# Prompt attention: value products on half the array each, four at once, and softmax sums from the row pass

## The reference, cut to what matters

```python
def fox_block(qi, cq, qpos, k, v, ck):
    scale = FOX_DIM ** -0.5                                   # FOX_DIM = 64, SEQ = 2048, 8 heads
    logits = jnp.einsum('bqhd,bkhd->bhqk', qi, k, preferred_element_type=jnp.float32) * scale
    logits = logits + cq[..., :, None] - ck[..., None, :]     # c: running sum of the log forget values
    mask = jnp.arange(k.shape[1])[None, :] <= qpos[:, None]
    logits = jnp.where(mask, logits, -jnp.inf)
    p = jax.nn.softmax(logits, axis=-1).astype(v.dtype)
    return jnp.einsum('bhqk,bkhd->bqhd', p, v)
```

## Time and profile before

| | |
|---|---|
| Median of 3 runs | 3781.91 us (3779.85 to 3783.17) |
| Profiled execution, own time | 3778.13 us |
| Its span | 3776.4 us |
| TensorE busy | 3628.9 us, 96% |
| VectorE busy | 1614.3 us, 43% |
| ScalarE busy | 1170.2 us, 31% |
| Mean granted TensorE clock | 0.988 of 2.4 GHz |

### The profile page before, as it was taken

How to read it: one execution, slowest core, us unless ns; L and a number is a source line. 1 busy time by engine, 2 the same in 40 slices (tenths; PEclk the granted TensorE clock), 3 DMA queues, 4 the chain that set the end, 5 groups by cost and what they waited for, 6 DMA issues and landing times. The chain is left out here.

```text
span 3776.4 us, 54542 instructions
## 1 busy us (share of the span) xinstructions
PE 3628.9 (96%) x20888; PEld 3168.2 (84%) x20888; DVE 1614.3 (43%) x3505; ACT 1170.2 (31%) x2318; POOL 337.4 (9%) x416
## 2 busy tenths in 40 slices
PE   8999999899999999998879999999999999999998
PEld 8999999777777677776668889999999999888886
DVE  4000377655554554444544444444444444432222
ACT  5122122334333333332223333333333333321111
POOL 3000000211211111121200000000000000000000
PEclk9999999999999999999979999999999999999999
DMA  4212322311221022015443421111111111432222
GB/s 158 70 62 64 83 73 70 91 29 43 58 51 40 25 62 47 19 55 179 162 153 121 129 72 44 46 46 46 46 46 46 46 46 35 153 126 81 81 81 68
DMA packets 328132, 278.90 MB, mean 74 GB/s; under 512 B 97219, under 2 KB 292915, under 8 KB 326894
## 3 DMA queue, kind: packets, MB, share of 16 engines
q1 hardware_dynamic: 318319, 258.03, 23.0%
q0 software_dynamic: 5216, 18.23, 1.4%
q10 hardware_dynamic: 4416, 0.14, 0.1%
HBM read 190.70 MB, written 85.65 MB: 73 GB/s over the span
## 5 line engine op out<-in xcount | busy, mean ns | idle before, releaser
L2627 PE MATMUL bank<-ffn_hn_hi,ffn_w_parts 128*128 128x436 f32 (+1 forms) x3520 | 986.4, 361 | 2.4 <-ACTq L2734 2.4
L2627 PEld LDWEIGHTS bank<-ffn_hn_hi,ffn_w_parts 128*128 128x128 f32 x3520 | 661.3, 188 | 39.1 <-issue 2.7
L2627 PE MATMUL bank<-ffn_hn_lo,ffn_w_parts 128*128 128x436 f32 (+1 forms) x1760 | 634.1, 360 | 0.0
L416 PE MATMUL bank<-in_xh,in_wh 128*128 128x436 f32 (+1 forms) x1280 | 356.4, 359 | 2.3 <-DVE in_wh L634 2.3
L2627 PEld LDWEIGHTS bank<-ffn_hn_lo,ffn_w_parts 128*128 128x128 f32 x1760 | 330.8, 188 | 19.3
L2661 PE MATMUL bank<-ffn_down_wa,ffn_g_hi 128*128 (+1 forms) x1224 | 328.6, 390 | 3.4 <-DVE ffn_g_lo L2956 3.4
L2763 ACT COPY ffn_raw<-bank 128x436 f32<-128x436 f32 (+1 forms) x220 | 110.3, 501 | 704.2 <-PE bank L2627 649.7
L1555 PE MATMUL bank<-heads_p_pT,heads_p_v 128*65 128x512 f32 (+3 forms) x640 | 286.4, 529 | 10.3 <-issue 9.8
L2890 DVE TENSOR_SCALAR ffn_hist<-ffn_raw 128x2 f32 (+2 forms) x264 | 44.9, 170 | 547.7 <-ACT ffn_acc L2767 544.9
L2661 PEld LDWEIGHTS bank<-ffn_down_wa,ffn_g_hi 128*128 128x128 f32 x1224 | 229.9, 188 | 52.7 <-DVE ffn_down_wa L2953 3.3
L1612 ACT ACTIVATE heads_p_pT<-bank 128x512 f32<-128x512 f32 (+1 forms) x320 | 170.1, 533 | 271.4 <-PE bank L1540 170.0
(11 more groups left out here) (419 smaller groups left out, 6232.5 us busy)
## 6 DMA issues: line engine op xcount, KB each, us to landing
ffn_w<-in_w_up_dram SPq DMA_DIRECT2D x44, 512.0 KB, 5.0
ffn_g_raw<-scratch_g SPq DMA_DIRECT2D x110, 192.0 KB, 2.3
scratch_g<-ffn_acc SPq DMA_DIRECT2D x88, 218.0 KB, 2.0
heads_s_k<-in_cache_fox_k_dram SPq DMA_DIRECT2D x8, 2048.0 KB, 13.5
heads_s_v<-in_cache_fox_v_dram SPq DMA_DIRECT2D x8, 2048.0 KB, 8.3
heads_d_qkvT<-scratch_gch SPq DMA_DIRECT2D x17, 768.0 KB, 5.6
ffn_y<-in_w_down_dram SPq DMA_DIRECT2D x22, 512.0 KB, 3.4
scratch_gch<-in_work SPq DMA_DIRECT2D x48, 218.0 KB, 1.9
```

What stands on the lines that cost most here:

```text
L416: mm = pe.matmul(bank[:, 4 + i % 2, 0:wide], a[:, k, :], b[:, k, col:col + wide], start=(k == 0 and m == 0), stop=(k == KD - 1 and m == 2))
L2627: mm = pe.matmul(bank[:, pair(n) + e, 0:width], w_parts[a][:, part, e, k, :], x[:, k, cols], start=(k == 0 and m == 0), stop=(k == KD - 1 ...
```

## The change

**Values.** `v` loses its column of ones and has 64 columns. The product of an even key block goes to PSUM partitions 0 to 63 and that of an odd block to partitions 64 to 127 of the same bank, so each uses 64 of the array's columns. `values_tensor` now issues four products in a row (`AT_ONCE`), after the fourth block's exponential. `pT` has eight buffers instead of three (`NPT`); they are lent by `Delta.S_s`, the running streams' states, whose load on SP now waits until the last row-bank use of `Prompt` is freed. `oT` has 128 rows; `turn_out` transposes 128x128 pieces, and `normalise` adds the two halves with a reduction over the turned bank before it multiplies. (In the first piece of a head only the even half has been written, so 64 rows are turned.)

**Sums.** The softmax denominator is taken from the row pass. The operands `q_both`, `q_hi`, `causal` and the exponentials' scale change sign, so that a tile's row minimum is the negated maximum and can serve as ScalarE's bias. After `row_max`, ScalarE exponentiates the same tile from PSUM into a scratch tile `junk`, with `accum_out` as its row sum, and frees the bank. `sums_vector` and `sums_scalar` (between its first two steps, `share = exp(rise)`) weigh the tiles' sums by exp of their distance to the group's maximum and take the reciprocal.

**Waits and times.** `row_free` becomes two semaphores, one for each bank. `SPEED` goes from 0.62 to 0.54 and the block's cost in `set_times` from 2.65e-3 to 1.81e-3 a column; `Prompt.end` goes from 974.9 to 897.6 units (the sum of `cost(G) / SPEED` over the 32 groups, plus 34.0), while `Delta`'s times stay. The last scaling of `Sample` on VectorE gets a due time 10.2 units later.

```diff
@@ Delta.sync
             if t == NC - 2:
+                sp.wait_ge(*self.prompt.freed(len(self.prompt.uses) - 1))
                 sp.dma_start(self.S_s[:].rearrange("p b h n -> p (b h) n"),
@@ Prompt
-    SPEED = 0.62
+    SPEED = 0.54
+    NPT, AT_ONCE = 8, 4
-        self.v = ph.sb("p_v", [P, 2, NB, FD + 1])
+        self.v = ph.sb("p_v", [P, 2, NB, FD])
-            return 2.65e-3 * sum(self.width(G, b) for b in range(self.blocks(G))) + 0.95e-3 * first + 1.6 + \
+            return 1.81e-3 * sum(self.width(G, b) for b in range(self.blocks(G))) + 0.95e-3 * first + 1.6 + \
+    def freed(self, r):
+        return self.s[f"row_free{r % 2}"], r // 2 + 1
@@ rows_tensor
-                mm = pe.transpose(self.row_bank(r)[:, i * (FD + 1):(i + 1) * (FD + 1)], self.oT[:, i * P:(i + 1) * P],
-                                  c["ident"][0:FD + 1, 0:FD + 1])
+                rows = slice(0, FD if G % self.NG == 0 and i == 0 else P)
+                mm = pe.transpose(self.row_bank(r)[:, i * P:i * P + rows.stop], self.oT[rows, i * P:(i + 1) * P],
+                                  ident[rows, rows])
...
-            after(pe, s["row_free"], r - 1)
+            if r >= 2:
+                pe.wait_ge(*self.freed(r - 2))
@@ values_tensor
-            yield at + 4.0
...
-            pe.wait_ge(s["p_ready"], u + 1)
-            pe.matmul(self.bank[0:self.FD + 1, self.out, BANK - wide:BANK], self.v[:, h % 2, b, :],
-                      self.pT[:, u % 3, BANK - wide:BANK], start=(b == 0), stop=(b == last)).then_inc(s["pv_mm"], 1)
+            if b % self.AT_ONCE != self.AT_ONCE - 1:
+                continue
+            yield at + 4.0
...
+            pe.wait_ge(s["p_ready"], self.first_key[G] + b + 1)
+            for n in range(first, b + 1):
+                half, cols = n % 2, slice(BANK - self.width(G, n), BANK)
+                mm = pe.matmul(self.bank[half * FD:(half + 1) * FD, self.out, cols], self.v[:, h % 2, n, :],
+                               self.pT[:, (self.first_key[G] + n) % self.NPT, cols], start=n < 2, stop=n >= last - 1)
+            mm.then_inc(s["pv_mm"], 1)
@@ rows_scalar
+            elif tag[0] == "s":
...
+                yield at + 2.6
...
+                act.wait_ge(s["top_step"], self.top_base[G] + i * (G % self.NG + 1) + j + 1)
...
+                nc.scalar.activation(self.junk[:, len(tiles) % 2, 0:wide], bank[:, 0:wide], ACT.Exp, scale=-1.0,
+                                     bias=self.low[:, G % 2, i, j:j + 1],
+                                     accum_out=self.part[:, G % 2, i, j:j + 1]).then_inc(self.free(r), 1)
@@ sums_vector
+            tt(rise, spread(self.top[:, a, :].unsqueeze(2), [P, 4, g + 1]), self.low[:, a, :, tiles], ALU.subtract) \
+                .then_inc(s["sum_step"], 1)
+            yield self.sums_at(G) + 3.0
+            dve.wait_ge(s["share_ready"], G + 1)
+            dve.wait_ge(*self.freed(self.use["s", G, 3, g]))
+            tt(share, share, part, ALU.mult).then_inc(s["sum_step"], 1)
+            dve.wait_ge(s["sum_step"], 4 * G + 2)
+            nc.vector.tensor_reduce(self.inv[:, G % 4, :], share, AX.X, ALU.add).then_inc(s["sum_step"], 1)
+            dve.wait_ge(s["sum_step"], 4 * G + 3)
+            nc.vector.reciprocal(self.inv[:, G % 4, :], self.inv[:, G % 4, :]).then_inc(s["sum_step"], 1)
@@ vector: row_max, normalise
             nc.vector.tensor_reduce(self.low[:, G % 2, i, j:j + 1], self.row_bank(r)[:, 0:self.row_width(G, i, j)],
-                                    AX.X, ALU.max).then_inc(s["row_free"], 1)
+                                    AX.X, ALU.min).then_inc(s["top_step"], 1)
...
-            nc.vector.reciprocal(self.inv[:, a, :], turned[:, :, FD]).then_inc(s["inv_ready"], 1)
...
-            tt(self.o[:, a], turned[:, :, 0:FD], spread(self.inv[:, a, :].unsqueeze(2), [P, 4, FD]), ALU.mult) \
-                .then_inc(s["row_free"], 1)
+            nc.vector.tensor_reduce(self.o[:, a, first:], turned[:, first:].rearrange("p n e d -> p n d e"), AX.X, ALU.add) \
+                .then_inc(self.free(r), 1)
+            dve.wait_ge(*self.freed(r))
+            tt(self.o[:, a, first:], self.o[:, a, first:], spread(inv[:, first:].unsqueeze(2), [P, 4 - first, FD]), ALU.mult) \
+                .then_inc(s["o_ready"], 1)
```

160 lines of the change are left out of this document (98 added, 62 removed).

## The result

The changed kernel takes **3835.9 us** (median of 4 runs, 3833.8 to 3838.9) against 3782.3 us before (4 runs): ratio **1.0142**, 95% interval [1.013, 1.0154]. It is slower by 54 us where I had forecast 41 us less. The FFN's first matmul moved from 1967.66 us to 2028.74, so all of it arises in the heads stage (59 us in the spans of the two profiled executions).

The account below looks back on a forecast made before the run. TensorE, busy 96% of the span, was taken as the bound. Terms -85 + 6 + 32 + 3 + 3 = -41 us against the profiled 3778.1 gave 3737, and with 3.8 to the median 3741 us; range 3698 to 3782.

Parts of the forecast that it names:

- Values, -85: Prompt's value products on TensorE: fours with overlapping halves on half the array save 85 us.
- strict-order rival: Value products: matmul passes go in strict order, so the term is -58 instead of -85, 3768 us; chance 0.1.
- Transposes, +6: Turning the output on TensorE: 120 of 128 pieces go from 65 to 128 columns, costing 6 us.
- Row-pass waits, +32: Row pass: TensorE waits longer for row banks now that ScalarE's exponential follows VectorE; 32 us, bounds 15 and 100.
- 28 + 14: Row pass: 34 existing waits each 0.83 us longer, 28 us; as many joining tiles at half the price, 14 us.
- upper bound of 100: Row-pass waits: a tile's exponential stands behind another ScalarE instruction, so some 70 tiles wait 1.4 us each.
- `4 products + 0.31`: Price of a value four on TensorE: its products' work plus 0.31 us for entering and leaving the narrow mode.
- End of the heads, +3: End of the heads stage: `Delta`'s last steps now end it alone, at a lower clock; +3 us, bounds -10 and +20.
- Key path +3: Key pass: a block's exponential can stand behind a row tile on ScalarE, delaying TensorE; 3 us (0 to 15).
- VectorE and ScalarE at nothing: Prompt's stretch: ScalarE's 230 us and VectorE's 48 us of added work leave neither a bound by its sum; no cost.
- The likeliest case: Whole kernel: the forecast of 3720 to 3760 us, given 0.55.
- last rival: Row bank: exponential behind a ScalarE copy awaiting later TensorE work; bank back after 3 us, slower beyond 73 us stalls; chance 0.12.

Follow-up runs that it names:

- the other run: Changed kernel with each value product over 128 array columns instead of 64, still in fours: 3923.6 us, ratio 1.0373.
- The stand-in with singles: Changed kernel without row exponentials, with the old timetable, value products on full width and issued one at a time: 3799.9 us, ratio 1.0044.
- The copy-out kernel: Changed kernel with VectorE copying the row tile to SBUF with the minimum, freeing the bank; ScalarE exponentiates the copy: 3779.5 us, ratio 0.9992.
- the kernels that shorten the hold: Changed kernel with VectorE copying the tile out to SBUF (3779.5 us), or ScalarE copying it first and VectorE taking the minimum from the copy (3768.9 us).
- speed 0.50 under a ScalarE-only hold: Changed kernel with ScalarE copying the tile first and alone holding the bank, plus SPEED 0.50 and last scaling at 15.0: 3745.6 us, ratio 0.99.
- twos: Value products in twos instead of fours: 3753.9 us without exponentials and with old timetable; 3761.4 us with VectorE copying out at speed 0.50.

## Why the prediction was wrong

The runs make a ladder from one kernel to the other, each step one edit (steps in us, from the ratios times 3782). Beside it stand three quantities of the profiled execution between 737 us and the FFN's first matmul. "Half rate" is half of the time at 1.2 GHz in the trace's clock record, the work lost to it (in each kernel TensorE was idle for 12 to 16 us of that time, so this hardly touches the steps). "Idle" is the time in which no matmul runs. "Work" is what is left of the length.

| Kernel | step | work | idle | half rate |
|---|---|---|---|---|
| Before | | 1109 | 95 | 27 |
| + all parts but those below, full width, singles | +17 | 1124 | 96 | 29 |
| + products in fours | +33 | 1135 | 112 | 39 |
| + fours side by side | -82 | 1051 | 115 | 40 |
| + row exponentials | +73 | 1059 | 155 | 63 |
| + new timetable (the change) | +13 | 1061 | 158 | 72 |

- **Values, -85: right.** The step measures -82 (-87 in the other run), and a full four 1.87 us with 0.2 more around it. The strict-order rival falls: it wanted 2.44.
- **Transposes, +6.** The stand-in with singles is 17 us slower than before. Not separated are the transposes, the small VectorE steps, and that its weights have 128 columns where the kernel before had 65; the last goes with the side-by-side step.
- **Row-pass waits, +32: the step that failed.** It measured +73 with the old times and +75 with the new. The waits themselves were near. With the old times a tile's weight load waits 42 us longer for its bank with the exponentials than without, as my 28 + 14 had it:

```profile
PEld bank L1504 <- DVE heads_p_low L1721: 21.1, 27, 2.0
```

```profile
PEld bank L1504 <- ACT heads_p_junk L1610: 62.6, 64, 2.7
```

The first line is of the kernel without exponentials, the second of the one with them. The sum of the waits is in part luck, for the hold was too short in my working: between these two kernels its mean grows by 1.03 us, from 1.97 to 3.00, and not by 0.83. ScalarE's two instructions take 0.89 us for a full tile (0.69 and 0.20) where I had 0.78, and in the changed kernel ScalarE starts on a tile 0.49 us after VectorE's end in the mean (the median is 0.04), as other work at times stands ahead on its queue. Not counted were the other users of the two banks (turned output, maxima, key copies), 13 us more. Of the 55 us in all, 40 are new idle time of TensorE, so "a quarter may take the place of idle time" was about right. But these 40 are little more than half of the 73. Another 24 are clock: I had no term for work done at 1.2 GHz in the prompt's stretch, because the kernel before had 1 us of it. The last 8 are work, and their cause stays open. My upper bound of 100 for the term did hold the 75; the value taken was at the wrong end of it.
- **Grouping by four, not in the sum: +33.** I priced the four as `4 products + 0.31` and not what it takes from its surroundings. Of the 37 us by the two traces, 11 are work as the trace counts it, 16 idle time and 10 clock.
- **End of the heads, +3, and the timetable.** The stage behind the last value product grew by 45 us, of which most was moved there (the last chunk of `Delta`); the new timetable costs 13 us net, inside the bound of 20.
- **Key path +3, VectorE and ScalarE at nothing.** The copy-out kernel bounds the price of ScalarE's work and its read-outs, apart from the hold, at 19 us.

The miss of 95 us adds up from the steps: 3 for the products, 11 for the transposes and what is not parted from them, 33 for the grouping, 38 for the exponentials (73 against 32 and 3) and 10 for the timetable (13 against 3).

The likeliest case fell. Of the last rival the mechanism came true, but it doesn't give the 3836 by itself: its 73 to 75 us are just where I had said that the time turns (73), so with my other terms they make 3782 to 3784, no change. What makes the kernel slower are the terms that stood in no sum on top of them, the grouping above all. The rival's chain through VectorE is in the timeline above, and the kernels that shorten the hold under nearly the same load get back 57 and 67 of the 75 us. How many of the 100 waits have that chain was not counted. The rival was given 0.12; the clock in the prompt's stretch and the grouping were in no case at all, so the upper end of 3782 was too low. A stall in a stretch where TensorE is busy 95% is not only its own length. What stays open: why the fours' work rises by 11 us at full width, what the 8 us of work in the exponentials' step are, and the larger gain of speed 0.50 under a ScalarE-only hold. An exponential and a maximum reading the bank at the same time was not tried.

## What to carry to other kernels

When a buffer is handed through a second in-order engine, price the hold by what stands ahead on *both* queues, count every user of the buffer, and expect TensorE's clock to charge for the gaps again (here 24 us beside 40 of idle time); let the first reader copy out (here 82 ns more) and give the buffer back. Price a grouping by a run that only groups: the duration of four products together showed nothing of the 33 us that it cost, and twos got idle time back but paid it in ways in and out. A planner's speed is to be set again after every such step, with the time behind the last unit of each body in view.

## What the hardware showed

- A column-tiled FP32 product on half the array overlaps its neighbour nearly in full: eight matmuls of 512 columns in 1.87 us, against 3.49 on the full width (1214.58 to 1218.07 in the kernel with full-width fours):

```profile
1214.58 3.65 PE L1577 MATMUL bank<-heads_d_S_s,heads_p_v 128*128 128x512 f32 x8
1218.07 1.05 PE L937 MATMUL bank<-heads_d_kb,heads_d_XT 128*128 128x128 f32 x8
```

- The halves run on independently. In the causal four from 1220.43 us the last product in program order has 128 columns, on the odd half; but the matmul that starts last, and ends last by the trace's modelled ends, has 256, on the even half:

```profile
1221.56 0.38 PE L1576 MATMUL bank<-heads_d_S_s,heads_p_v 128*64 128x256 f32 x1
```

The Trainium skill's page "TensorE: Matmul & The Clock Gate", Part 3, section "The mechanism", says that matmuls are "pc-monotone in start AND end" and that one increment on the last is therefore sound. The starts here speak against the first half. The reader of this bank, which waits for the 128-column matmul's increment, started at 1221.99, behind both; so the trace doesn't show an early release.
- At the lower clock (granted 0.54 and 0.61 in the windows above) a full four takes about twice as long, 3.61 us from 1126.74 to 1130.35 instead of 1.87.

```profile
1126.74 3.68 PE L1576 MATMUL bank<-heads_d_S_s,heads_p_v 128*64 128x512 f32 x8
1130.35 0.69 PE L1556 MATMUL bank<-heads_p_q_both,heads_p_k_hi 128*128 128x384 f32 x1
```
